# Where the SBUF tensors of a two-block layer kernel lie: small tensors ahead of the large ones

## The reference

```
def reference(x, ...):
    x = first_block(x, ...)            # one hybrid layer
    return second_block(x, ...)        # two layers and a final norm

# hybrid layer
z = rms_norm(x) @ w_in                                # 18 column tiles of 128, and 16 low-rank columns
o_gla = gated linear attention, 4 heads, chunks of 64; rms_norm; times silu(gr)
o_swa = sliding-window attention, 8 heads, 2 kv heads, window 128, ALiBi, sinks
x = x + concat(o_gla, o_swa) @ w_out
u = causal_dwconv(rms_norm(x) @ w_up)                 # three taps; 2 x 2816 features
x = x + (silu(a) * b) @ w_down

# second block: layer 0 dilated window attention, layer 1 differential attention
h = h + mix(rms_norm(h))
y = relu(rms_norm(h) @ w_in);  h = h + (y * y) @ w_out      # 4096 features
return rms_norm(h)
```

## Time and profile before

| | |
|---|---|
| median of three runs | 1901.91 us (1892.46 to 1902.54) |
| the profiled execution's own time | 1902.54 us |
| its span, first to last instruction | 1900.7 us |
| PE busy | 1834.1 us (96%) |
| DVE, ACT, POOL busy | 955.4, 749.3, 720.4 us (50%, 39%, 38%) |
| mean granted TensorE clock | 0.970 of full speed |
| DMA | 167.44 MB, mean 88 GB/s |

### The profile page before, as it was taken

One profiled execution on the slowest core, in us unless ns is written; L12 is line 12 of the kernel. 1 busy time (PEld: TensorE's weight loads), 2 busy tenths in 40 slices (PEclk: granted clock), 3 DMA queues, 4 the chain that ended last, 5 costly groups with the idle time before them and its releaser, 6 DMA issues.

```text
span 1900.7 us, 24762 instructions
## 1 busy us (share of the span) xinstructions
PE 1834.1 (96%) x8344; PEld 1463.5 (77%) x8344; DVE 955.4 (50%) x1641; ACT 749.3 (39%) x1224; POOL 720.4 (38%) x312
## 2 busy tenths in 40 slices
PE   7898899999999999999999999999999999999997
PEld 4676677888888877876888888887777778888886
DVE  4744434555541135465535261657777773526164
ACT  3533234555542243433423232435555442323242
POOL 2221014444444433332444444434444344444443
PEclk9899779999999999998999999999999999999998
DMA  4211002323323422221223233232232222333232
GB/s 146 78 56 46 22 22 89 104 95 95 99 93 100 139 97 63 84 78 58 89 94 96 98 99 92 96 116 88 104 106 76 67 84 95 98 99 99 89 100 77
DMA packets 48054, 167.44 MB, mean 88 GB/s; under 512 B 5155, under 2 KB 6451, under 8 KB 47830
## 3 DMA queue, kind: packets, MB, share of 16 engines
q1 hardware_dynamic: 47894, 166.43, 27.2%
q10 hardware_dynamic: 96, 0.15, 0.1%
HBM read 164.31 MB, written 2.24 MB: 88 GB/s over the span
## 4 chain that ended last, share of the span: by engine, by line
PE 88%; DVE 5%; ACT 3%; issue 3%; DMA 0%; DVEq 0%; ACTq 0%; SPq 0%
PE bank L434 15%; PE bank L435 15%; PE bank L440 14%; PE bank L749 12%; PE bank L681 4%; PE bank L682 4%; PE bank L688 4%; PE bank L727 2%; PE bank L726 2%; PE bank L732 2%; PE bank L984 1%; PE bank L1013 1%; PE bank L648 1%; DVE tmp L2177 1%; PE bank L830 1%
## 5 line engine op out<-in xcount | busy, mean ns | idle before, releaser
L370 POOL TENSOR_TENSOR w_lo<-stage,w_hi 128x1024 fp32r<-128x1024 f32 x284 | 686.7, 2419 | 1086.9 <-ACT w_hi L1118 663.7
L1118 ACT ACTIVATE w_hi<-stage 128x1024 fp32r<-128x1024 f32 x284 | 299.3, 1055 | 390.3 <-PE bank L435 291.5
L434 PE MATMUL bank<-xn_hi,w_hi 128*128 128x512 f32 x688 | 280.0, 407 | 12.9 <-ACT w_hi L1118 10.4
L435 PE MATMUL bank<-xn_lo,w_hi 128*128 128x512 f32 x688 | 273.8, 398 | 0.0
L434 PE MATMUL bank<-arena,w_hi 128*128 128x512 f32 x608 | 238.0, 391 | 3.3 <-DVE x L1576 1.6
L435 PE MATMUL bank<-arena,w_hi 128*128 128x512 f32 x608 | 236.7, 389 | 0.0
L2177 DVE TENSOR_TENSOR tmp<-tmp,rstd 128x512 f32<-128x512 f32 x64 | 151.5, 2367 | 112.0 <-ACT tmp L1526 112.0
L440 PE MATMUL bank<-xn_hi,w_lo 128*128 128x512 f32 x688 | 172.8, 392 | 0.0
L434 PEld LDWEIGHTS bank<-xn_hi,w_hi 128*128 128x128 f32 x688 | 133.0, 193 | 50.7 <-ACT w_hi L1118 10.4
L440 PE MATMUL bank<-arena,w_lo 128*128 128x512 f32 x608 | 160.6, 389 | 0.0
L435 PEld LDWEIGHTS bank<-xn_lo,w_hi 128*128 128x128 f32 x688 | 133.4, 194 | 28.4 <-issue 1.2
(11 more groups left out here) (275 smaller groups left out, 2704.5 us busy)
## 6 DMA issues: line engine op xcount, KB each, us to landing
stage<-weights SPq DMA_DIRECT2D x284, 512.0 KB, 3.5
bias<-table SPq DMA_DIRECT2D x11, 896.0 KB, 6.1
out<-z SPq DMA_DIRECT2D x8, 256.0 KB, 2.1
x<-x_in SPq DMA_DIRECT2D x1, 1024.0 KB, 9.0
bias<-swa_table SPq DMA_DIRECT2D x4, 256.0 KB, 3.6
con<-consts SPq DMA_DIRECT2D x1, 640.0 KB, 11.8
bias<-table SPq DMA_DIRECT2D x5, 128.0 KB, 3.5
par<-params SPq DMA_DIRECT2D x1, 515.0 KB, 4.3
```

The lines of the kernel that those rows point to most:

```text
L370: nc.gpsimd.tensor_tensor(w_lo[:, p_], stage[:, p_], w_hi[:, p_].bitcast(F32), ALU.subtract).then_inc(lo_ready, 1)
L434: pe.matmul(G[p_][:], w_hi[:, p_, k], hi[:, k], start=(first and k == ks[0]), stop=False)
L435: mm = pe.matmul(G[p_][:], w_hi[:, p_, k], lo[:, k], start=False, stop=False)
L1118: act.activation(w_hi[:, p_], stage[:, p_], ACT.Copy).then_inc(hi_ready, 1)
```

## The change

The declarations of the SBUF tensors stand in another order. `par` and `con` now come right after `w_lo`, then `bias`, `tmp`, `rstd`, `rstd_h` and the small tensors, and the block of `ff_space`, `z`, `qkv`, `prob`, `v_tok` with `arena` and `v_split` comes last.

```
@@ -109,19 +109,12 @@
         w_lo = sb("w_lo", [P, 2, KD, P], F32R)
-        with nc.sbuf_tensor("ff_space", [P, 2 * KD, S], F32):
-            with nc.sbuf_tensor("z", ...) as z, nc.sbuf_tensor("qkv", ...) as qkv, \
-                    nc.sbuf_tensor("prob", ...) as prob, nc.sbuf_tensor("v_tok", ...) as v_tok:
-                pass
-        arena = sb("arena", [P, 2 * NF1, S], F32R)
-        v_split = sb("v_split", [P, 2, 2, NQ, P], F32R)
+        par = sb("par", [P, N_PAR])
+        con = sb("con", [P, N_CON])
         bias = sb("bias", [P, 2, 2, EXT])
         tmp = sb("tmp", [P, 4, S])
         rstd = sb("rstd", [P, S])
         rstd_h = sb("rstd_h", [P, S])
-        con = sb("con", [P, N_CON])
-        glr_w = sb("glr_w", [P, 2, KD * 32], F32R)
...
         small = sb("small", [P, 128])
+        glr_w = sb("glr_w", [P, 2, KD * 32], F32R)
         grp = sb("grp", [P, 6, NQ, 3])
         lhe = sb("lhe", [P, 2, NQ, 6])
         lse15 = sb("lse15", [P, 2, NQ, 15])
-        par = sb("par", [P, N_PAR])
+        (the block of ff_space, arena and v_split, as it was)
```

More of the change, by code:

```diff
@@ L111, in program @@
         w_lo = sb("w_lo", [P, 2, KD, P], F32R)
-        with nc.sbuf_tensor("ff_space", [P, 2 * KD, S], F32):
-            with nc.sbuf_tensor("z", [P, N_IN, S], F32) as z, nc.sbuf_tensor("qkv", [P, 2, 3, S], F32) as qkv, \
-                    nc.sbuf_tensor("prob", [P, 2, 2, S], F32) as prob, \
-                    nc.sbuf_tensor("v_tok", [P, 2, 2, NQ, P], F32) as v_tok:
-                pass
-        arena = sb("arena", [P, 2 * NF1, S], F32R)
-        v_split = sb("v_split", [P, 2, 2, NQ, P], F32R)
+        par = sb("par", [P, N_PAR])
+        con = sb("con", [P, N_CON])
         bias = sb("bias", [P, 2, 2, EXT])
@@ L135, in program @@
         lse15 = sb("lse15", [P, 2, NQ, 15])
-        par = sb("par", [P, N_PAR])
+        with nc.sbuf_tensor("ff_space", [P, 2 * KD, S], F32):
+            with nc.sbuf_tensor("z", [P, N_IN, S], F32) as z, nc.sbuf_tensor("qkv", [P, 2, 3, S], F32) as qkv, \
+                    nc.sbuf_tensor("prob", [P, 2, 2, S], F32) as prob, \
+                    nc.sbuf_tensor("v_tok", [P, 2, 2, NQ, P], F32) as v_tok:
+                pass
+        arena = sb("arena", [P, 2 * NF1, S], F32R)
+        v_split = sb("v_split", [P, 2, 2, NQ, P], F32R)
         ff_hi, ff_lo, zr = arena[:, 0:KD], arena[:, KD:2 * KD], arena[:, 2 * KD:2 * KD + N_IN]
```

## The result

The changed kernel takes 1916.59 us (median of 6 runs, 1908.34 to 1917.94) against 1900.74 for the kernel before (6 runs, 1892.46 to 1902.54). The ratio of the two is 1.009, 95% interval 1.0061 to 1.0118: slower by 0.9%, or 15.9 us between the medians. I had forecast no change, 1902 us, and a range up to 1916. Its profiled execution took 1911.13 us (before: 1902.54).

A forecast was written before the change was run, and what follows sets the result against it. The prediction took PE, busy for 96% of the span, to bound the kernel. All terms were taken as 0, so their sum was 0 and the forecast 1902 us, no change, with an 8-in-10 range from 1888 to 1916 us.

The forecast's parts named there:

- What bounds the kernel: Whole kernel: PE bounds it, busy 96% of the span; its pace did not depend on which tensor was read.
- Moving operands in `arena`: 2928 PE matmuls reading arena at shifted addresses: loss taken as 0, bounds 0 to 19.6 us.
- The estimate of 6.7 ns: Upper bound per arena matmul: a slice touching 33 pieces of 64 bytes, not 32, would cost 6.7 ns more.
- The rule of the Trainium skill: SBUF lines are 16 bytes, so a 32-byte shift keeps arena slices on line bounds: 0, not 19.6 us.
- The rest of the stream: 1216 PE matmuls reading z, qkv, prob, con, tmp and bias: at most 8.1 us more, taken as 0.
- DVE, ACT, DMA: Shifted starts on these engines: each taken as 0; DVE within 1 us, ACT at most 1.4, DMA at most 0.5.
- PE pays (slower): Rival: the 2928 arena matmuls pay for alignment, 19.6 us, up to 27.7, giving 1922 us; chance 0.16.
- PE gains (faster): Rival: shifting moving slices against weights stops their reads meeting, up to 35.7 us off, 1867 us; chance 0.09.
- POOL and DVE part: Rival: DVE's long tmp product beside POOL's split speeds up as tmp moves, giving 1897 us; chance 0.03.
- The low clock: Rival: PE's early low-clock spell falls differently; a median on the quick clock gives 1892 us; chance 0.09.

The follow-up runs named there:

- e3_all_32: The kernel before with a 32-byte gap ahead of x, so moving operands and weights alike start 32 bytes past a multiple of 64; ratio 1.0013.
- e4_w_32: The kernel before with 32-byte gaps on both sides of the weights, so w_hi and w_lo alone start 32 bytes past a multiple of 64; ratio 1.0187.

## Why the prediction was wrong, point by point

- *What bounds the kernel.* Right: only PE's time counted, and the step that asked which tensor the pace depends on led to the right pair of stretches.
- *Moving operands in `arena`.* This is the step that failed: "I take 0", on the ground that the weight load of `par` and the place of `arena` had made no difference. The runs showed a price of 6.7 ns for each matmul whose moving slice stands 32 bytes further than its weights modulo 256: the term is 16.8 us by the busy time of the 2928 matmuls, of which 2640 are on `w_hi` and `w_lo` (2640 times 6.7 is 17.7) and the other 288 had partners that moved with them. That is inside the bounds of 0 and 19.6 us, and near the upper one. The rows could not carry it: before the change all big operands lay at 128 modulo 256, so every row of the pace showed one phase only, however far apart the tensors were; and the load of `par` (L578) was looked at for its own 185 ns, while what changes is the pitch of the 512-column stream beside it. The text had called this unknown; the value chosen for it was the comfortable end.
- *The estimate of 6.7 ns.* The size was right to the tenth, 226.7 to 233.4 ns, and the mechanism behind it was wrong. A slice that touches one piece more would pay wherever it starts at 32, which `e3_all_32` refutes, and would not pay when only the weights move, which `e4_w_32` refutes. That 16 columns at 2.4 GHz make the same 6.7 ns proves nothing by itself.
- *The rule of the Trainium skill* on 16-byte lines ("Advanced Engine Details and Errata", "Memory Cachelines") gave 0 for this term; the measured 16.8 us decide otherwise. Its lines may be 16 bytes long, but the pitch of matmuls depends on starts in steps up to 256 bytes, so the rule does not cover this.
- *The rest of the stream.* The 1216 other matmuls, bounded at 8.1 us, cost nothing that can be seen. Most have both operands in tensors that all went from 128 to 160 modulo 256 together (`z`, `qkv`, `prob`, `con`, `tmp`, `bias`), and many are shorter than 512 columns; which of the two spares them was not tested.
- *DVE, ACT, DMA.* Right: 750 and 2349 ns on DVE, 299.3 us of `w_hi` copies on ACT before and after, `stage` loads at 3.5 us. The buckets took 14.7 us to land in place of 12.9, more than the tenth allowed for, and landed well before their reader all the same.
- *PE pays (slower), 0.16.* Right in place, size and test (355 to 345, 443 unchanged), wrong in its chance and its cause.
- *PE gains (faster), 0.09.* It named the two reads of PE as a pair whose relative start matters, which is what was found, but with the sign reversed: the old layout was the good phase. The 13.3 ns of 226.7 above the 213.3 of 512 columns stay in every pair tried at 2.4 GHz.
- *POOL and DVE part.* Wrong, as held likely: `tmp` moved by 89056 bytes and its long product stayed at 2349 ns. In the changed kernel's trace all 64 of the long products run beside a split on POOL and none of the 64 `tmp<-tmp` does, which answers the doubt left there. That agrees with the port rule of the Trainium skill ("SBUF — State Buffer", "Who interferes with whom") that the prediction named.
- *The low clock.* The 10 us between executions are real on both sides and shift neither median against the other; they cost the reading of the profiled execution 6 us.

## What to carry to other kernels

An address is part of a matmul's cost: in a stream of fp32r matmuls with 128 weight columns and 512 moving ones, put weights and moving operands on the same start modulo 256, and that start on a multiple of 32 (equal starts of 4 and of 16 bytes were slow, 238.6 and 230.1 ns), and pad an odd-sized tensor rather than let it shift what comes behind. When rows show that a place makes no difference, look first whether they ever differed in what the change alters; a bound that no row narrows should keep its weight. A count of matmuls in two stretches of one trace, one touched and one not, shows 3% where the medians need many runs to show 0.9%.

## What the hardware showed that I had not expected

PE's pitch for 128 x 128 by 512 at 2.4 GHz is 226.7 ns at its best and lies between 227 and 239 ns for other starts, with no other engine at work. At 1.2 GHz it is 427 ns, whether the starts fit or are 32 bytes apart. The starts of weights and slice count together, not the place of either: 226.7 at distances of 4096, 65536 and 98304 bytes. For one pair, (0, 192), the pitch depends on what ran before, 228.9 or 233.3 ns. With 256 moving columns and 128 weight columns the order is turned round: 119.5 ns at equal starts, 113.6 with the weights 64 bytes further.
